# Query and key pieces as 512- and 256-column products, their halves added by VectorE

## What is computed

```
proj = x @ w_in;  c_q, c_kv, k_idx, w_idx = split(proj)   # c_q: 512, c_kv: 256 columns
c_q, c_kv = rms_norm(c_q), rms_norm(c_kv)
q  = c_q @ w_uq                   # 16 heads of 128        -> q_t
q_lat = q . w_uk;  s = q_lat . kv_sel                      # the kernel: k_t = w_uk . c_kv, s = q_t . k_t
p = softmax(s * scale over the chosen keys)
o_lat = p . kv_sel;  o = o_lat . w_uv                      # the kernel: values = c_kv . w_uv
return concat(o) @ w_out
```

## Time and profile before

| | us |
|---|---|
| median of three runs | 954.66 |
| the profiled execution, its own time | 954.25 |
| its span, first to last instruction | 952.5 |
| PE busy in the span | 947.6 (99%) |
| DVE busy | 633.4 (67%) |
| ACT busy | 442.7 (46%) |
| POOL busy | 40.5 (4%) |

### The profile page before, as it was taken

How to read it: one execution, slowest core, us unless ns; L and a number is a source line. 1 busy time by engine, 2 the same in 40 slices (tenths; PEclk the granted TensorE clock), 3 DMA queues, 4 the chain that set the end, 5 groups by cost and what they waited for, 6 DMA issues and landing times.

```text
span 952.5 us, 12291 instructions
## 1 busy us (share of the span) xinstructions
PE 947.6 (99%) x4514; PEld 794.6 (83%) x4514; DVE 633.4 (67%) x1010; ACT 442.7 (46%) x572; POOL 40.5 (4%) x41
## 2 busy tenths in 40 slices
PE   9999999999999999999999999999999999999998
PEld 8999988888888888888888888888888888888886
DVE  5778566588776677777776677677775454544556
ACT  5676764362544444444444444444444344343450
POOL 0105530000000000000000000000000000000000
PEclk9999999999999999999999999999999999999999
DMA  9835225583365555554455555555457465564632
GB/s 364 323 136 178 99 79 185 212 345 142 112 218 201 182 207 184 190 206 176 176 190 210 207 186 191 205 178 202 171 211 295 140 231 184 163 240 149 228 126 88
DMA packets 27984, 183.57 MB, mean 193 GB/s; under 512 B 3120, under 2 KB 3376, under 8 KB 8496
## 3 DMA queue, kind: packets, MB, share of 16 engines
q1 hardware_dynamic: 27920, 183.12, 53.7%
q0 software_dynamic: 32, 0.00, 0.0%
HBM read 181.01 MB, written 2.10 MB: 192 GB/s over the span
## 4 chain that ended last, share of the span: by engine, by line
PE 99%; DMA 0%; DVE 0%; ACT 0%; SPq 0%; issue 0%
PE acc L1289 82%; PE acc L1227 5%; PE acc L1151 4%; PE acc L1426 2%; PE acc L1261 1%; PE tp L1340 1%; PE tp L1275 1%; PE tp L1353 1%; DMA raw<-in_x_w 0%; PE tp L1365 0%; PE tp L1364 0%; PE tp L1366 0%; PE tp L1382 0%; PE tp L1519 0%; PE tp L1516 0%; PE tp L1195 0%
## 5 line engine op out<-in xcount | busy, mean ns | idle before, releaser
L875 DVE TENSOR_TENSOR w_lo<-raw,w_hi 128x1024 fp32r<-128x1024 f32 (+1 forms) x283 | 335.3, 1194 | 242.4 <-ACT w_hi L623 240.5
L623 ACT ACTIVATE w_hi<-raw 128x1024 fp32r<-128x1024 f32 (+1 forms) x276 | 285.8, 1036 | 403.1 <-PE acc L1289 401.1
L1289 PE MATMUL acc<-w_hi,act_t 128*128 128x512 f32 x1344 | 414.1, 389 | 0.0
L1289 PEld LDWEIGHTS acc<-w_hi,act_t 128*128 128x128 f32 x1344 | 252.4, 188 | 52.2
L1289 PE MATMUL acc<-w_lo,act_t 128*128 128x512 f32 x672 | 261.6, 389 | 0.0
L1289 PE MATMUL acc<-w_hi,hid_t 128*128 128x512 f32 x672 | 207.3, 389 | 0.0
L1289 PEld LDWEIGHTS acc<-w_hi,hid_t 128*128 128x128 f32 x672 | 126.2, 188 | 26.2
L1289 PEld LDWEIGHTS acc<-w_lo,act_t 128*128 128x128 f32 x672 | 126.2, 188 | 26.2
L1289 PE MATMUL acc<-w_lo,hid_t 128*128 128x512 f32 x336 | 130.8, 389 | 0.0
L1022 DVE STREAM_TRANSPOSE turned<-hid 32x128 f32<-32x128 f32 x352 | 106.6, 303 | 5.7
L1289 PEld LDWEIGHTS acc<-w_lo,hid_t 128*128 128x128 f32 x336 | 63.1, 188 | 12.9
(11 more groups left out here) (180 smaller groups left out, 742.3 us busy)
## 6 DMA issues: line engine op xcount, KB each, us to landing
raw<-in_w_gu SPq DMA_DIRECT2D x88, 1024.0 KB, 4.8
raw<-in_w_down SPq DMA_DIRECT2D x32, 1024.0 KB, 4.8
raw<-in_w_out SPq DMA_DIRECT2D x16, 1024.0 KB, 4.8
raw<-in_w_down SPq DMA_DIRECT2D x16, 768.0 KB, 4.2
raw<-in_x_w SPq DMA_DIRECT2D x14, 552.0 KB, 7.1
raw<-in_w_uq SPq DMA_DIRECT2D x4, 1024.0 KB, 5.9
raw<-in_w_ukv SPq DMA_DIRECT2D x4, 1024.0 KB, 4.8
ln_rows<-in_ln_rows SPq DMA_DIRECT2D x4, 1024.0 KB, 7.7
```

Of the source, the lines that this page charges most:

```text
L623: act.activation(w_hi[:, (2 * slot + half) % RING, 0:n], raw[:, slot, first:first + n], ACT.Copy).then_inc(hi_done, 1)
L875: dve.tensor_tensor(w_lo[:, h, 0:n], raw[:, slot, first:first + n], w_hi[:, h, 0:n], ALU.subtract).then_inc(lo_done, 1)
L1289: last = pe.matmul(acc[:, bank0 + t, :], lhs[:, k, x, t * P:(t + 1) * P], part[:, w, n * GC:(n + 1) * GC], start=(start and x == 0 and par ...
```

## The change

The pieces for queries and keys made in the head loop (6, 8, 9, 10, 12, 13 and 14) are computed by a new function `wide_tile`. It gives each tile a bank of its own. W_hi is multiplied with x_hi and x_lo at once, as one product of 512 columns (x_hi in the bank's first half, x_lo in its second), and W_lo with x_hi as one of 256 columns that accumulates onto the first half. Over the k steps the order is high, low, low, high, high, low, low, high. ACT copies the second halves of two banks to `q_t` or `k_t` (`take_half`, counted in the new semaphore `half_taken`), and DVE adds the first halves of the same two banks onto them in place (`add_piece`) and adds two to `taken`. On ACT `take_half` stands where `take_piece` stood, behind the Exp of its step; on DVE `add_piece` stands at the end of its step, behind `lo_static`. A query piece now uses two banks and a key piece four (`M_LATE`), so the bank numbers shift, and `out_k` waits for `M_OUT`. Pieces 0 to 5, 7, 11 and 15 keep their products. `take_piece` waits for `taken` to reach its first bank number.

```diff
--- before.py
+++ after.py
@@ -109,16 +109,22 @@
 M_PIECE = (1, 1, 2, 2)
-M_PER_GROUP = sum(M_PIECE)
+
+M_LATE = (2, 2, 4, 2)
 M_GROUP = 4
-M_OUT = M_GROUP + GROUPS * M_PER_GROUP
+
+
+def first_bank(s):
+
+    return M_GROUP + sum((M_PIECE if i < EARLY else M_LATE)[i % 4] for i in range(s))
+
+
+M_OUT = first_bank(4 * GROUPS)
 M_DOWN = M_OUT + COL_GROUPS
-
-def first_bank(s):
-
-    g, j = divmod(s, 4)
-    return M_GROUP + M_PER_GROUP * g + sum(M_PIECE[:j])
+HALVES_BEFORE = {s: first_bank(s) - sum(M_LATE[i % 4] for i in range(EARLY, s) if i % 4 < 3)
+                 for s in range(EARLY, 4 * GROUPS)}
+
@@ -293,6 +299,7 @@
         acc_full = sem("acc_full")
         acc_t0_full = sem("acc_t0_full")
         taken = sem("taken")
+        half_taken = sem("half_taken")
         logits_full = sem("logits_full")
         relu_done = sem("relu_done")
         score_step = sem("score_step")
@@ -501,6 +508,7 @@
                 g, j = divmod(s, 4)
                 m = first_bank(s)
+                act.wait_ge(taken, m)
                 if j < 2:
                     take(m, q_t[:, g % 2, 2 * j:2 * j + 2, :])
                 elif j == 2:
@@ -509,6 +517,17 @@
                 else:
                     for t in range(TOK):
                         take(m + t, values[g % 3][:, t, :])
+
+            def take_half(s):
+
+                g, j = divmod(s, 4)
+                m = first_bank(s)
+                dst = k_t[:, g % 2, :, :] if j == 2 else q_t[:, g % 2, 2 * j:2 * j + 2, :]
+                for n in range(M_LATE[j] // 2):
+                    bank = (m + 2 * n) % 4
+                    act.wait_ge(acc_full, m + 2 * n + 2)
+                    act.activation(dst[:, 2 * n:2 * n + 2, :], acc[:, bank:bank + 2, S:2 * S],
+                                   ACT.Copy).then_inc(half_taken, 2)
             for k in range(KD):
                 hi_in(k)
@@ -610,7 +629,10 @@
                                        bias=row_min[:, s % 2, t:t + 1],
                                        accum_out=row_sum[:, s % 2, t:t + 1]).then_inc(exp_done, 1)
                 if s in PIECE_OF:
-                    take_piece(PIECE_OF[s])
+                    if PIECE_OF[s] % 4 == 3:
+                        take_piece(PIECE_OF[s])
+                    else:
+                        take_half(PIECE_OF[s])
                 if s in SPLIT_OF:
                     hi_static(SPLIT_OF[s])
@@ -831,6 +853,18 @@
             dve.wait_ge(mask_done, 2)
             dve.tensor_tensor(key_bias[:, 0:P], key_bias[:, 0:P], masked[:], ALU.max).then_inc(bias_done, 1)
             dve.wait_ge(bias_done, 1)
+
+            def add_piece(s):
+
+                g, j = divmod(s, 4)
+                m = first_bank(s)
+                dst = k_t[:, g % 2, :, :] if j == 2 else q_t[:, g % 2, 2 * j:2 * j + 2, :]
+                for n in range(M_LATE[j] // 2):
+                    bank = (m + 2 * n) % 4
+                    half = dst[:, 2 * n:2 * n + 2, :]
+                    dve.wait_ge(taken, m + 2 * n)
+                    dve.wait_ge(half_taken, m + 2 * n + 2 - HALVES_BEFORE[s])
+                    dve.tensor_tensor(half, half, acc[:, bank:bank + 2, 0:S], ALU.add).then_inc(taken, 2)
             for s in range(HEADS + 4):
                 if s >= 4:
@@ -861,6 +895,8 @@
                     lo_static(2 * R_GROUP + 9)
                 elif s - 1 in SPLIT_OF:
                     lo_static(SPLIT_OF[s - 1])
+                if s in PIECE_OF and PIECE_OF[s] % 4 < 3:
+                    add_piece(PIECE_OF[s])
                 if POOL_NORM < s <= HEADS:
                     dve.wait_ge(inv_done, s)
                     dve.wait_ge(prob_done, 2 * (s - 1))
@@ -1240,12 +1276,39 @@
                     for t in range(TOK):
                         turn(t, range(KQ, KQ + KV + 1))
+            def wide_tile(v, n, kts, act_tiles, m):
+
+                hi_, lo_ = split_place(v)
+                bank = m % 4
+                pe.wait_ge(taken, m - 3)
+
+                def high(k):
+                    return pe.matmul(acc[:, bank, :], hi_[:, v % RING, (n * kts + k) * P:(n * kts + k + 1) * P],
+                                     act_tiles[:, k, :, :], start=(k == 0), stop=(k == kts - 1), skip_group_check=True)
+
+                def low(k):
+                    pe.matmul(acc[:, bank, 0:S], lo_[:, v % RING, (n * kts + k) * P:(n * kts + k + 1) * P],
+                              act_tiles[:, k, 0, :], start=False, stop=False, skip_group_check=True)
+
+                high(0)
+                for k in range(0, kts, 2):
+                    low(k)
+                    low(k + 1)
+                    last = high(k + 1)
+                    if k + 2 < kts:
+                        high(k + 2)
+                last.then_inc(acc_full, 1)
+
             def piece(s, tiles=range(4)):
                 j = s % 4
                 m = first_bank(s)
                 v = 2 * R_GROUP + s
                 pe.wait_ge(lo_done, v + 1)
+                if j < 3 and s >= EARLY:
+                    for n in range(M_LATE[j]):
+                        wide_tile(v, n, KV if j == 2 else KQ, ckv_t if j == 2 else cq_t, m + n)
+                    return
                 if j < 3:
                     for n in tiles:
                         if j < 2 and n < 2:
@@ -1314,7 +1377,7 @@
                 h = ks[0] // OUT_K
                 if ks[0] == 0 and g <= 1:
-                    pe.wait_ge(taken, M_OUT - 2 + 2 * g)
+                    pe.wait_ge(taken, M_OUT)
                 elif ks[0] == 0:
                     pe.wait_ge(res_done, TOK * (g - 1))
                 if ks[0] % OUT_K == 0:
```

## The result

Seven runs of the changed kernel have a median of 957.97 us (956.96 to 958.72), seven of the kernel before 954.81 (954.22 to 955.14). The ratio is 1.0031, with a 95% interval of 1.0022 to 1.0040: slower by 3.2 us, where +1.85 was forecast and 957.6 was the range's upper end. The seven runs are of two kinds. Three took 956.96 to 957.29, with a mean granted clock of 1.000; four took 957.97 to 958.72, with 0.998. The profiled run is of the second kind: 958.06 us, span 956.3. Of the executions of the kernel before, one took 1364.27 us at a granted clock of 0.655 and is left out as slow; the others lie between 954.08 and 955.76.

The account below looks back on a forecast made before the run. PE, busy 947.6 of 952.5 us, was taken to bound the kernel. A 2.2 us wait less 0.36 saved gave +1.85 us, 954.66 to 956.5, with a range of 955.2 to 957.6.

Parts of the forecast that it names:

- the sum: Whole kernel: 2.2 us of wait less 0.36 saved, +1.85 us, so 954.66 becomes 956.5.
- the clock falls in the gap: Rival: PE falls back to 1.2 GHz after 2 idle us before piece 7, adding 1.65: 958.2 us; chance 0.04.
- products twice as long after the gap: Sign that the forecast is wrong: PE's products take double time after the idle stretch before piece 7.
- The wait at piece 7: Step 1: PE waits for DVE's first addition of piece 6, behind ACT's late half copy; 2.2 us late (2.1 to 2.3).
- The saving: Changed query and key pieces on PE: 0.06 us each, six count, 0.36 us saved (bounds -0.3 and 1.7).
- The other waits: Pieces 11 and 15, `out_k`'s first product and a key piece's third tile: all four cost nothing.
- The margin at piece 11: Steps 4 and 5: piece 10's first addition ends at least 0.4 us before piece 11 needs it.
- No wait at piece 7: Rival: first addition ends by 84.0, so PE does not wait and only the saving is left: 954.3 us; chance 0.05.
- the mixed order is much faster: Rival: changed pieces near their columns' time, 0.29 us saved each, 1.7 in six: total +0.5, 955.2 us; chance 0.07.

Follow-up runs that it names:

- filled: The changed kernel with ten products of 512 columns, whose result nobody reads, put before piece 7 on PE: 956.93 us, ratio 1.0022.
- the run with one wait: The changed kernel with Exp's table loaded early, and the second semaphore waits of DVE's first addition and PE's piece 7 moved earlier or dropped: 955.56 us, ratio 1.0007.
- the kernel with early copies: The changed kernel with Exp's table loaded early, piece 6's half copies before the first Exp and its additions before DVE's low parts: 954.94 us, ratio 1.0002.

## Why the prediction was wrong

**The step that failed is that the sum has no term for the clock.** It let the granted clock stay at 1.00 behind the gap, and "the clock falls in the gap" was a rival with a chance of 0.04 and a time of 958.2, outside the range. The runs showed that the fall is the more frequent case, and that it costs some 1.57 us: 4.59 us for piece 7 in place of 3.02. The prediction's own sign of it, "products twice as long after the gap", is what the profile shows. I argued from "rows 2 show 1.00 throughout; but they hold no gap at all" and still kept the chance at 0.04: rows without a gap bore out nothing, and the one row that had PE idle, its start, showed the lower level. (By its products' times; the profile's clock column reads 1.00 there. The other half of that comparison isn't in the line of rows 11, whose mean of 381 ns counts overlapping products. It comes from the chain, where the scores' four records, 768 columns in all, take 0.66 us, so 0.22 for 256.) What the runs put there, by PE's idle time before piece 7: none (filled), no fall in 11 runs; 0.8 to 0.9 us, none in 22; 2.2 us, a fall in 11 of 17; 3.7 us, in 5 of 5.

Some of the agreement is luck. The rival's 958.2 is also the median of the seven slower runs of twelve, but it stood on a wait worked out too short: 957.0 and 1.57 make 958.6. And the median of the changed kernel's first seven runs, 957.97, is the fastest of its four slower ones; with one more run of the first kind in its place it would have been about 957.3, inside the range, and the sum would have lacked the clock all the same.

**The wait at piece 7** was right in place, cause and sequence: half copies behind Exp, addition behind them, PE released when `taken` passes 13. It was mis-sized: 2.47 us, where 2.2 (2.1 to 2.3) was worked out. Of the 0.27, 0.10 is that ACT's copies began at 84.88 in place of 84.78:

```profile
84.88 1.06 ACT L529 ACTIVATE k_t<-acc 128x512 f32<-128x512 f32 x2
```

ACT was that late from its copy of piece 5 on, which begins at 80.18 in place of 80.08. The rest is that the addition began 0.12 us after the copy's end and PE 0.14 after the addition's, where the prediction took 0.04 and 0.05. Both engines wait for two semaphores there. For PE the run with one wait shows that the second one makes the difference (0.04); for DVE it is argued from the 0.05 us of L866 in its queue, and no run tests it. In the runs whose clock stayed up the whole came to 957.0 (median of five), 0.5 above the forecast.

**The saving** was 0.04 a piece, not 0.06, and 0.24 in six: the products of 512 stay at the value pieces' 232 ns and the narrow ones at 118. The term was mis-sized by 0.12. The Trainium skill (TensorE: Matmul & The Clock Gate, section "Back-to-back issue gap") has N / 2.4 + 2.5 ns, which that page gives for a single product by itself. The prediction's 2.60 us a piece by it is an estimate, and the changed kernel's trace, a stream of products, does not agree with it either: 2.80 to 2.82.

**The other waits.** Pieces 11 and 15 and the output products did not wait, as worked out. The addition takes 0.70 us in the chain, where 0.69 was worked out. The margin at piece 11 is thinner than the 0.4 us of the prediction: in the changed kernel the first addition of piece 10 ends at 103.73 and the first product of piece 11 is recorded from 104.01, 0.28 us later, of which PE's start behind an addition takes 0.14. In the kernel with early copies 0.1 us was lost there.

**The rivals.** "No wait at piece 7" and "the mixed order is much faster" fell, the second to 2.80 to 2.82 us a piece in either order.

## What to carry to other kernels

Where a piece of work takes all the banks, the next piece waits for the first bank's copy; look on the copying engines for what stands before that copy in the step where they are latest, here a table load. Price a gap of the matrix engine twice: by its length, and by what the clock takes back after it, and give the second a real chance when no row shows a gap of that length harmless. Joining narrow products into wide ones at the same columns was worth little here: 8 fewer of 24 gave 0.04 of 2.85 us.

## What was unexpected of the hardware

The clock fell not in the gap but after work had begun again, in the three profiled runs that show a fall 0.8, 1.3 and 0.4 us after it (gaps of 2.24, 2.21 and 3.74 us), and it stayed at 1.2 GHz for 3.4 us in each. It did not fall in every run: the same kernel, with the same gap of 2.24 or 2.25 us, lost 1.57 us in one profiled run and nothing in the other. What decides between the two in a given run stays open.

A second semaphore that PE had to wait for cost 0.10 us at the moment of release: 0.14 against 0.04 us from DVE's end to PE's start.
